# A two-block sequence kernel in fp32 on one core: the feed-forward's down products in a phase of their own, by seven block products in place of eight

## The reference

```python
def conv_glu(hn, w_up, conv_f_w, conv_f_b, w_down):          # first block
    up = hn @ w_up
    gate = jax.nn.gelu(causal_dwconv(up[..., :D_FF], conv_f_w, conv_f_b), approximate=False)
    return (gate * up[..., D_FF:]) @ w_down

y = (jax.nn.silu(u @ w_gate[l]) * (u @ w_up[l])) @ w_down[l]  # second block
h = h + rms_norm(y, g_ffn_post[l])
```

## Time and profile before

| | us |
|---|---|
| median of 3 runs | 2813.38 (2813.02 to 2814.61) |
| the profiled execution, from its first to its last instruction | 2812.4 |
| TensorE busy, share | 2756.6, 98% |
| TensorE weight loads | 2267.9, 81% |
| VectorE busy | 1763.2, 63% |
| GpSimd busy | 1365.9, 49% |
| ScalarE busy | 1027.8, 37% |
| matmuls | 13,262 |
| DMA | 191.31 MB, mean 68 GB/s |

### The profile page before, as it was taken

How to read it: one execution, slowest core, us unless ns; L and a number is a source line. 1 busy time by engine, 2 the same in 40 slices (tenths; PEclk the granted TensorE clock), 3 DMA queues, 4 the chain that set the end, 5 groups by cost and what they waited for, 6 DMA issues and landing times.

```text
span 2812.4 us, 36491 instructions
## 1 busy us (share of the span) xinstructions
PE 2756.6 (98%) x13262; PEld 2267.9 (81%) x13262; DVE 1763.2 (63%) x1889; ACT 1027.8 (37%) x1638; POOL 1365.9 (49%) x774
## 2 busy tenths in 40 slices
PE   8999999999999999999999999999999999999999
PEld 6888788888788888888887777778876888888886
DVE  7988552336976667776845446883369656555556
ACT  4256531332422222222413435553456222222224
POOL 4322212214666667666566331543254765566663
PEclk9999999999999999999999999999999999999999
DMA  4101322011111111112322110432023111111113
GB/s 151 38 23 38 105 97 83 31 67 46 46 52 45 52 52 48 63 52 82 128 92 96 46 38 17 140 114 82 23 96 118 49 56 60 48 47 55 51 56 134
DMA packets 72274, 191.31 MB, mean 68 GB/s; under 512 B 7792, under 2 KB 8048, under 8 KB 71408
## 3 DMA queue, kind: packets, MB, share of 16 engines
q1 hardware_dynamic: 61920, 157.12, 16.7%
q10 hardware_dynamic: 10256, 32.86, 3.2%
HBM read 172.65 MB, written 17.30 MB: 68 GB/s over the span
## 4 chain that ended last, share of the span: by engine, by line
PE 57%; issue 23%; POOL 12%; DVE 4%; ACT 2%; DMA 1%; POOLq 0%; ACTq 0%; DVEq 0%; SPq 0%
PE products L651 20%; PE products L1111 8%; PE others L1111 7%; PE others L1157 5%; PE products L1157 5%; POOL w_lo L559 4%; POOL w_lo L502 2%; POOL w_raw L577 1%; POOL w_raw L575 1%; PE others L651 1%; PE products L1047 1%; DVE work L2427 1%; DMA w_raw<-wstream 1%; POOL w_raw L566 1%; POOL part_sum L571 1%
## 5 line engine op out<-in xcount | busy, mean ns | idle before, releaser
L559 POOL TENSOR_TENSOR w_lo<-w_raw,w_hi 128x512 fp32r<-128x512 f32 x328 | 464.5, 1422 | 442.1 <-ACT w_hi L1897 441.1
L1897 ACT ACTIVATE w_hi<-w_raw 128x512 fp32r<-128x512 f32 x328 | 207.1, 633 | 815.9 <-PE products L1111 209.6
L499 POOL TENSOR_TENSOR w_hi<-w_raw,small 128x1024 fp32r<-128x1024 f32 x54 | 111.1, 2058 | 583.9 <-PE products L651 326.4
L651 PE MATMUL products<-act_hi,w_hi 128*128 128x512 f32 x864 | 346.9, 402 | 1.4 <-DVE act_lo L2383 1.3
L651 PE MATMUL products<-act_lo,w_hi 128*128 128x512 f32 x864 | 337.5, 391 | 0.0
L651 PE MATMUL products<-act_hi,w_lo 128*128 128x512 f32 x864 | 337.5, 391 | 0.0
L502 POOL TENSOR_TENSOR w_lo<-w_raw,w_hi 128x1024 fp32r<-128x1024 f32 x94 | 253.0, 2691 | 144.6 <-ACT w_hi L2226 140.4
L651 PEld LDWEIGHTS products<-act_hi,w_hi 128*128 128x128 f32 x864 | 162.9, 189 | 42.0 <-issue 7.3
L651 PEld LDWEIGHTS products<-act_hi,w_lo 128*128 128x128 f32 x864 | 162.7, 188 | 35.0
L651 PEld LDWEIGHTS products<-act_lo,w_hi 128*128 128x128 f32 x864 | 163.2, 189 | 31.4 <-issue 0.2
L745 PE MATMUL products<-act_hi,w_hi 128*128 128x512 f32 x408 | 167.0, 409 | 7.4 <-DVE act_lo L3329 4.7
(11 more groups left out here) (555 smaller groups left out, 6928.0 us busy)
## 6 DMA issues: line engine op xcount, KB each, us to landing
w_raw<-wstream SPq DMA_DIRECT2D x155, 512.0 KB, 3.3
w_raw<-wstream SPq DMA_DIRECT2D x248, 256.0 KB, 2.6
work<-xT ACTq DMA_DIRECT2D x16, 512.0 KB, 8.8
parked<-work ACTq DMA_DIRECT2D x8, 512.0 KB, 3.0
work<-parked ACTq DMA_DIRECT2D x8, 512.0 KB, 5.1
parked<-work ACTq DMA_DIRECT2D x2, 2048.0 KB, 8.7
work<-parked SPq DMA_DIRECT2D x8, 512.0 KB, 7.6
out<-work SPq DMA_DIRECT2D x16, 256.0 KB, 2.3
```

What stands on the lines that cost most here:

```text
L499: pool.tensor_tensor(w_hi[:, slot, :], w_raw[:, slot, :], zeros, ALU.add)\
L559: pool.tensor_tensor(ring_lo[slot], source, ring_hi[slot].bitcast(F32), ALU.subtract).then_inc(s(signal), 1)
L651: last = pe.matmul(out[:, c], a[:, ws, w], x[:, k, c], start=(k == 0 and i == 0), stop=(k == KT - 1 and i == 2))
L1897: act.activation(ring_hi[slot], source, ACT.Copy).then_inc(s("parts_high"), 1)
```

## The change

The ten chunks are worked in two phases. In the first, the pair loop, a pair's hidden tile is stored to a DRAM tensor (`parked_hidden`, 20 tiles of 512 KB) and no down product is made. Three of a pair's products for the up tile and two for the gate accumulate in the same PSUM bank as an earlier product (`start=False`); ScalarE copies the bank out in between, three copies a pair in place of one, and VectorE has four additions a pair in place of seven. The ring of the pair loop has four slots.

In the second phase the down product of ten chunks is made by seven block products. There are two rounds of five chunks; a round has seven *steps*, a step has five *units*, one for each chunk, and a unit is one block product of 12 matmuls (4 output tiles x 3) of 128 features of the contraction by 512 tokens. The five units of a step accumulate in four PSUM banks; after a step VectorE adds its four banks to the running sum (`step_added`). Steps 0, 5 and 6 use blocks of the weights as loaded; steps 1 to 4 need a sum of blocks, made for every unit by GpSimd. The hidden tiles are loaded again; their high parts are made on ScalarE, low parts and sums (steps 1 to 4) on VectorE. Weights and hidden tiles of a unit have rings of four slots each. The last chunk's down product stays plain. At the start of the second feed-forward the third group of low parts comes last of the three, and the order of the first pair's products changes accordingly.

```diff
+ROUNDS = 2
+ROUND = BLOCKED // ROUNDS
+STEPS = 7
+STEP_UNITS = STEPS * ROUND
+UNITS = ROUNDS * STEP_UNITS
+SUMS = 4 * BLOCKED
+LAST_HIGH, LAST_LOW = 8, 10
+FF_EVACUATED = 4 + 8 * BLOCKED + 4 + 4 * STEPS * ROUNDS + 8
+
 STAGES = [("z1", 17, 17), ("out1", 8, 8), ("k1", 8, 8), ("v1", 8, 2), ("q1", 8, 9), ("xo1", 8, 8),
...
+                    pe.wait_ge(s("evacuated"), first - 3)
+                    part_product(1, 1, out(1), *lower_half)
+                    part_product(1, 2, out(2), *lower_second)
+                    pe.wait_ge(s("evacuated"), first - 2)
+                    pe.wait_ge(s("factor_lo"), factors + 8)
+                    part_product(1, 3, out(3), *difference[1])
+                    pe.wait_ge(s("factor_lo"), factors + (12 if name == "ffn2" else 8))
...
+                def pair(c, j, after_first=False):
+
+                    n = 7 * j
+                    chain_, other, alone = (bank(m) for m in pair_banks[j])
+                    if not after_first:
+                        pe.wait_ge(s("evacuated"), of.evacuated(c, 4 * j - 4))
+                    part_product(c, n + 1, chain_, *lower_half)
+                    if after_first:
+                        pe.wait_ge(s("evacuated"), of.first_evacuated + 2)
+                    part_product(c, n + 2, alone, *lower_second)
+                    pe.wait_ge(s("parts_copied"), of.copied(c, 3 * j + 1))
+                    part_product(c, n + 3, chain_, *difference[1], start=False)
+                    if after_first:
+                        pe.wait_ge(s("evacuated"), of.first_evacuated + 5)
+                    part_product(c, n + 4, other, *difference[0])
+                    pe.wait_ge(s("parts_copied"), of.copied(c, 3 * j + 2))
+                    part_product(c, n + 5, chain_, *third, start=False)
+                    pe.wait_ge(s("parts_copied"), of.copied(c, 3 * j + 3))
+                    part_product(c, n + 6, other, *upper_second, start=False)
+                    pe.wait_ge(s("evacuated"), of.evacuated(c, 4 * j + 2))
+                    part_product(c, n + 7, chain_, *upper_half, start=False, done=2)
+
+                def down_unit(u):
+
+                    r, s_, i = unit_of(u)
+                    g, slot, x = STEPS * r + s_, down_slot(u), u % 4
+                    pe.wait_ge(s("parts_split"), of.down_high(u))
+                    pe.wait_ge(s("factor_lo"), of.factor_low(u))
+                    for o in range(4):
+                        if not i:
+                            pe.wait_ge(s("evacuated"), of.evacuated(BLOCKED, 4 * (g + 1)) if g < 2 else of.added(4 * (g - 2) + o + 1))
+                        w = slice(o * P, (o + 1) * P)
+                        fresh = s_ in (0, 1, 3) and i == 0
+                        for m, (a, v) in enumerate(((down_hi, factor_hi), (down_hi, factor_lo), (down_lo, factor_hi))):
+                            last = pe.matmul(step_bank(g, o), a[slot][:, w], v[x], start=(fresh and m == 0),
+                                             stop=(i == ROUND - 1 and m == 2), skip_group_check=True)
+                    last.then_inc(s("product_quarters"), 1 + (8 * BLOCKED - UNITS if u == UNITS - 1 else 0))
...
-                def chunk(c):
-
+                first_pair()
+                pair(1, 1, True)
+                with pe.Fori(2, FC) as c:
                     pair(c, 0)
                     pair(c, 1)
-                    pe.wait_ge(s("ff_g_lo"), of.hidden(c, 0))
-                    pe.wait_ge(s("parts_copied"), of.copied(c, 2))
-                    for n in range(4):
-                        pe.wait_ge(s("parts_split"), of.split(c, 15 + n))
-                        down_half((14 + n) % 3, n, lambda o: (down_slots[o % 4], of.evacuated(c, (6, 10, 14, 14, 15, 16, 17, 18)[o])),
-                                  lambda k: g_hi[:, k, :], lambda k: g_lo[:, k, :])
-
-                chunk(1)
-                with pe.Fori(2, FC) as c:
-                    chunk(c)
...
+                def down_low(u):
+
+                    source, slot = part[u - UNITS] if u >= UNITS else down_source(name, *unit_of(u)[1:]), down_slot(u)
+                    pool.wait_ge(s("parts_high"), of.down_high(u))
+                    low_, high_ = (down_lo[slot], down_hi[slot]) if u >= UNITS else (by_o(down_lo[slot]), by_o(down_hi[slot]))
+                    pool.tensor_tensor(low_, source, high_.bitcast(F32), ALU.subtract).then_inc(s("parts_split"), 1)
+
+                chunk(1, True)
+                with pool.Fori(2, FC) as c:
+                    chunk(c)
+                for u in range(UNITS + 4):
+                    if u + 1 < UNITS and 1 <= unit_of(u + 1)[1] <= 4:
+                        down_sum(*unit_of(u + 1))
+                    down_low(u)
...
+                    pair(c, 1)
+                pair(FC - 1, 0)
+                pair(FC - 1, 1, True)
+                factor_high(0)
+                for u in range(UNITS):
+                    down_high(u)
+                    if u:
+                        factor_high(u)
+                    if u == 5:
+                        gate(BLOCKED, 1)
+                    if u == LAST_HIGH:
+                        last_high(0)
...
+                def step_added(g):
+
+                    r, s_ = g // STEPS, g % STEPS
+                    o0, half = ((0, 0), (0, 0), (0, 1), (4, 1), (4, 1), (0, 1), (4, 0))[s_]
+                    dve.wait_ge(s("product_quarters"), of.unit(ROUND * (g + 1) - 1))
+                    if g:
+                        dve.wait_ge(s("evacuated"), of.added(4 * g))
+                    elif not conv_tiles:
                         dve.wait_ge(s("mem_in"), 144)
...
+                scaled(BLOCKED, 1)
+                for u in range(4, UNITS):
+                    if u % ROUND == 2:
+                        step_added(u // ROUND - 1)
+                    factor_low(u)
+                    if u == 6:
+                        hidden(BLOCKED, 1)
+                    if u == LAST_LOW:
+                        last_low(0)
+                        last_low(1)
+                step_added(STEPS * ROUNDS - 1)
...
```

More of the change, by code:

```diff
@@ L576, in parts @@
+                        pool.tensor_tensor(part[1], part_sum[:, :], part[1], ALU.subtract).then_inc(s("parts_summed"), 1)
                         low(c, n + 4)
[L577 removed]
                         low(c, n + 5)
                         low(c, n + 6)
+                        if first and not pair:
+                            pool.wait_ge(s("factor_made"), of.factors_made + 8)
                         low(c, n + 7)
[L581 to L582 removed]
@@ new lines, in pair @@
+                def pair(c, j, last=False):
+                    n = 7 * j
+                    copied(c, j, 0)
+                    high(c, n + 4)
+                    high(c, n + 5)
+                    copied(c, j, 1)
+                    high(c, n + 6)
+                    gate(c if j else c + (-1), 1 - j)
+                    copied(c, j, 2)
+                    high(c, n + 7)
+                    if not last:
+                        for m in range(3):
+                            high(*((c + 1, m + 1) if j else (c, n + 8 + m)))
```

712 lines of the change are left out of this document (426 added, 286 removed).

## The result

| | before | changed |
|---|---|---|
| median of the runs, us | 2813.2 | 2836.45 |
| lowest to highest | 2812.51 to 2814.61 | 2834.84 to 2840.25 |
| profiled execution's span, us | 2812.4 | 2833.0 |
| matmuls on TensorE | 13,262 | 13,022 |

The ratio is 1.0082, with a 95% interval from 1.0067 to 1.0096: the kernel became 0.8% slower, with 240 fewer matmuls. The forecast was 2828.5 us, slower, in a range from 2789 to 2856.

A forecast was written before the change was run, and what follows sets the result against it. The prediction took TensorE's row of instructions as the bound: 2812.4 - 54.4 + 67 + 2.5 = 2827.5 us, and 1.0 us from profiled execution to median made 2828.5 us, range 2789 to 2856.

The forecast's parts named there:

- The matmuls: Down product: 1920 matmuls become 1680, so 240 fewer at 0.227 us each, -54.4 us.
- The pair loop: Pair loop: 18.4 of 19.0 us of shared GpSimd and VectorE work a pair fits, cost 0; bound 20 us.
- The turns: Down phase: GpSimd and VectorE alternate on two-SBUF-input instructions, 1.70 us a turn; units with sums take 3.40 us, 13.6 us a round.
- 6 of lead: Down phase: rings of four slots let a round spend about 6 us of work made ahead against its waits.
- VectorE's additions: Down phase: four bank additions (2.4 us) delay unit 2 of each step with sums by 2.3 us; bounds 0 and 2.4.
- The store and the loads: Tiles stored to and loaded from DRAM arrive in time, cost 0; one late would cost some 3 us, once.
- the down phases' 67 us: Waits in the two down phases: 16.8 us a round, four rounds, +67 us; bounds 30 and 93 us.
- The second start: Second feed-forward's first pair: product 3 now waits for both sets of low parts, one product (2.72 us) behind the wait, +2.5 us.
- The first start: First feed-forward: short waits for GpSimd go, VectorE's conv chain gives about as much back; 0, give or take 2 us.
- Case 2: Down phase: VectorE's additions cost nothing and only the alternation with GpSimd binds, 2791.5 us, faster; chance 0.18.
- its sign: Down-phase waits of under 12 us a round would show that additions cost nothing and only the engines' alternation binds.
- Case 4: Waits send TensorE to its low clock: ten such waits, 16 us on top, 2844.5 us; chance 0.12.

The follow-up runs named there:

- e1: Changed kernel with VectorE's forty factor sums of each feed-forward left out, waits kept: 2788.65 us, ratio 0.9912 to the kernel before.
- e9: Changed kernel with GpSimd's forty weight sums of each feed-forward left out, VectorE's kept: 2777.22 us, ratio 0.9857 to the kernel before.
- e6: Changed kernel without VectorE's additions to the output tiles for the second round's first six steps, both feed-forwards: 2835.64 us, ratio 1.0064 to the kernel before.
- e5: Changed kernel with the first lower tiles loaded ahead of later hidden halves, and one semaphore no longer shared: 2832.45 us, ratio 1.0056 to the kernel before.
- e2: Changed kernel with the last chunk's high copies and low parts moved from units 8 and 10 to 60 and 62: 2828.97 us, ratio 1.0052 to before.
- e8: Changed kernel with both engines' sums and VectorE's additions placed by tables, last chunk's parts at units 62 and 65: 2795.4 us, ratio 0.9922 to before.

## Why the prediction was right, and where it was not

**The matmuls, -54.4: right.** 13,022 are there, and 0.2267 us each at both stages.

**The pair loop, 0: right.** TensorE has work for 300.00 of 300.00 us. The conv chain does stretch under GpSimd's turns (2.08 us for a conv step at 910.04, where the earlier trace rows has 1.28), but fits.

**The turns: right**, in size, 1.70, 1.77 and 3.40 us, and in the second rounds in place: waits in steps 1 to 4, the longest at unit 2 of a step, none in 0, 5 and 6. In the first rounds step 0 has the wait for the late tile as well, at unit 4. e1 and e9 show the turns to be the cause of most of the waits. Without additions a round costs 10.8 us (e6), where 13.6 less 6 of lead gives 7.6: the lead is worth less than 6 us.

**VectorE's additions, "2.3 us a step, near the full price": wrong.** They cost 1.3 us a round (e6), not 9.2. The prediction had named the reason at its lower bound ("if GpSimd uses the free port meanwhile") and chose against it, because GpSimd's low part needs ScalarE's copy, which stands behind VectorE. That wait occurs, 1.91 us at 1274.62, but behind one of four groups of additions only, and there VectorE has the turn to itself and catches up; behind the other three GpSimd had its copy in time. So a plain round cost 12.1 us and not 16.8.

**The store and the loads, "Cost 0": wrong.** "Were one late, some 3 us, once" was the right kind of thing and too small: twenty tiles asked for within 20 us are 10.5 MB, 26 us at the 409 GB/s of the earlier trace rows, and GpSimd's first sum, ahead of unit 4's low part, needs the sixteenth and seventeenth of them. TensorE waited 5.2 and 4.5 us. e5 gives 1.2 and 4.2 us back by the order of the loads.

**Left out: the last chunk's two low parts of 128x1024**, behind each other on VectorE at unit 10, in turns 4.5 us. Moved, they give 3.0 and 3.5 us (e2), with the cold stretch behind the wait. They were in the change and in its order, and were not priced. The first rounds are 12 to 13 us worse than the second; e2 and e5, each alone, give back 4 and 8 us of that in sum (3.0 + 1.2, 3.5 + 4.2); the rest stays open.

So the down phases' 67 us came out as 75, with the common round overestimated by 4.7 us four times, and 25 us missing in the first rounds. The errors nearly cancelled: that the sum was off by only 8 us is partly luck.

**The second start, +2.5.** 10.5 us above the matmuls where the loop as a whole had 6.8, so +3.7: right in kind, low by 1.2 us. (The terms that it names, 2.72 less 0.2 and 0.4, make 2.1 and not 2.5.) TensorE's wait went from 3.70 to 7.39 us. That "both sets end at the same" time holds in the main: the second set ended at 2180.6, 7.3 us later, of which 6.6 us is the shift of the whole feed-forward's start. The first start, "0, give or take 2": 6.9 against 9.6, which held the loop's other waits as well.

**Rivals.** Case 2 (faster, additions nearly free) had the right mechanism for the additions, and the second rounds' 12.1 us stand just at its sign of under 12 us a round. Its time was wrong all the same: 75 us and not 30, since the lead was worth less and 25 us came from what no case held. Case 4, the clock: the long waits did send it to 1.2 GHz. The windows of the changed kernel:

```profile
1134.00:1136.00 2.00, 2.00 (x6) 1.61 (x5) 2.00 (x2) 0.00 (x0) 2.00 (x2) 0.51 0.00 0
1162.00:1166.00 4.00, 4.00 (x11) 3.13 (x10) 4.00 (x5) 1.15 (x2) 3.82 (x3) 0.50 0.00 0
```

Behind the waits of 5.19 and 4.84 us, and two like them in the second feed-forward, 8 to 14 matmuls each start 0.43 us apart; behind waits of 1.7 us and less none do. Some 40 matmuls by 0.2 us are 8 us in all, inside the 75, and not 16 on top; the mean clock of the span is 0.991. The Trainium skill, TensorE: Matmul & The Clock Gate (HAM oscillation) describes short bursts of matmuls with waits of microseconds between them, each burst starting at the low clock. The four long waits agree with it; the some fifty short ones are not such waits, and none of them was followed by slow matmuls.

## What to carry to other kernels

Before trading TensorE's work for that of VectorE and GpSimd, add up the two-SBUF-input instructions of both as one resource, stage by stage and not over the kernel: here a round held 93.5 us of it (55 pairs of 1.70 us) under 95.2 us of matmuls, and still 12 us were lost because twenty sums stood in twenty units in a row. That the rings of four slots leave too little lead is the likely other half; their length was not varied. Where such a stage comes out slower, move the work within its due times before giving the change up: the same instructions, spread out, turned 0.8% slower into 0.8% faster (e8). And list every instruction that the changed order has ahead of the first uses in a stage, the once-only ones too; a common unit priced to a tenth of a microsecond doesn't help where 4.5 us stand once in the way.

## What the runs showed of the hardware that was not expected

While one engine waits, the other has the turn to itself. Near the end of GpSimd's wait of 7.92 us for a load, VectorE made three sums and low parts 0.60 us apart, where in turns they take 1.70 each. So what a wait of GpSimd costs TensorE can't be read from its length: e5 took 2.9 us off GpSimd's waits in the first feed-forward and 2.6 in the second, and the down phases got 1.2 and 4.2 us shorter. For the same cause 2.4 us of VectorE's PSUM additions cost 0.2 us a step. The two-turn pattern isn't a fixed price per instruction but a price for being busy together.

Not tried: whether the additions stay as cheap with longer rings. Open: how the rest of the first rounds' 25 us divides over the last tile pair's gating, its product and the late tiles.
